# Head norms one half tile later, picks spread, and a bias table of 16 copies in a fused decoder layer

## What is computed

```
n = rmsnorm(h, g_mix)
q, k, v, qi, ki, wi, qb, kb, vb, gb, rb, uc, vc = split_proj(n @ w_in)
q, k = rmsnorm(q, q_norm_g), rmsnorm(k, k_norm_g)          # per head of 128
o_a  = attention over the top 64 (prompt) or 65 (samples) keys by indexer score,
       logits = q.k / sqrt(128) + rel_bias[rel_bucket(distance)]
o_b  = rmsnorm(gla(qb, kb, vb, log_sigmoid(gb @ w_gate_b + b) / 16)) * silu(rb)
o_c  = gelu(uc) * (w_spatial @ rmsnorm(gelu(vc)) + b_spatial)
h = h + concat(o_a, o_b, o_c) @ w_out
h = h + (silu(n2 @ w_ffn_gate) * (n2 @ w_ffn_up)) @ w_ffn_down
h = h + sigmoid(n3 @ w_ple_gate) * (p @ w_ple_proj)
```

## Time and profile before

| | |
|---|---|
| median of 3 runs | 1432.46 us (1432.43 to 1432.93) |
| profiled execution | 1431.66 us |
| its span | 1430.0 us |
| TensorE busy | 1409.9 us (99%) |
| VectorE busy | 850.1 us (59%) |
| ScalarE busy | 584.8 us (41%) |
| GpSimd busy | 111.8 us (8%) |
| moved by DMA | 237.95 MB |

### The profile page before, as it was taken

The page is one execution under the profiler, slowest core; times in us unless marked ns, Lnnn a source line. Parts: engine busy times, 40 slices in busy tenths (PEclk is TensorE's granted clock), DMA queues, the critical chain, the costliest instruction groups (busy, mean ns, idle before and its releaser), DMA issues.

```text
span 1430.0 us, 28384 instructions
## 1 busy us (share of the span) xinstructions
PE 1409.9 (99%) x10630; PEld 1383.3 (97%) x10630; DVE 850.1 (59%) x1173; ACT 584.8 (41%) x708; POOL 111.8 (8%) x160
## 2 busy tenths in 40 slices
PE   7999999999999999999999999999999999999999
PEld 7988888999999999999999999999999999999998
DVE  6568765655777555555554444555555556666654
ACT  7365554375433433333333333333333333335332
POOL 2023102210222000000000000000000001111000
PEclk9999999999999999999999999999999999999999
DMA  8766434443654545445445556554545545556553
GB/s 299 170 213 200 157 118 137 133 140 109 243 175 159 171 160 165 165 159 169 159 147 166 166 162 193 167 162 162 164 160 172 161 133 164 165 167 199 166 164 116
DMA packets 76503, 237.95 MB, mean 166 GB/s; under 512 B 13536, under 2 KB 15104, under 8 KB 76072
## 3 DMA queue, kind: packets, MB, share of 16 engines
q1 hardware_dynamic: 71136, 223.54, 48.9%
q0 software_dynamic: 3536, 11.46, 2.4%
q10 hardware_dynamic: 1784, 2.32, 1.0%
HBM read 231.35 MB, written 5.86 MB: 166 GB/s over the span
## 4 chain that ended last, share of the span: by engine, by line
PE 92%; DVE 3%; ACT 2%; DMA 2%; issue 1%; SPq 0%; DVEq 0%; ACTq 0%
PE acc L469 29%; PE acc L471 29%; PE acc L470 29%; DMA w_raw<-in_w_in 1%; DVE w_lo L435 1%; PE px L1530 1%; ACT w_hi L429 0%; PE px L1498 0%; ACT rl_s L729 0%; PE px L1479 0%; DMA proj<-in_xT 0%; PE px L469 0%; PE px L471 0%; PE px L470 0%; ACT L745 0%
## 5 line engine op out<-in xcount | busy, mean ns | idle before, releaser
L435 DVE TENSOR_TENSOR w_lo<-w_raw,w_hi 128x1024 fp32r<-128x1024 f32 (+2 forms) x448 | 510.5, 1144 | 332.4 <-ACT w_hi L429 323.6
L429 ACT ACTIVATE w_hi<-w_raw 128x1024 fp32r<-128x1024 f32 (+2 forms) x448 | 441.8, 989 | 570.2 <-PE acc L471 552.8
L469 PE MATMUL acc<-n_hi,w_hi 128*128 128x288 f32 x1664 | 492.8, 296 | 0.0
L470 PE MATMUL acc<-n_lo,w_hi 128*128 128x288 f32 x1664 | 490.9, 295 | 0.0
L471 PE MATMUL acc<-n_hi,w_lo 128*128 128x288 f32 x1664 | 489.2, 294 | 0.0
L471 PEld LDWEIGHTS acc<-n_hi,w_lo 128*128 128x128 f32 x1664 | 313.2, 188 | 0.0
L470 PEld LDWEIGHTS acc<-n_lo,w_hi 128*128 128x128 f32 x1664 | 312.2, 188 | 0.1
L469 PEld LDWEIGHTS acc<-n_hi,w_hi 128*128 128x128 f32 x1664 | 311.8, 187 | 0.1
L469 PE MATMUL acc<-x_hi,w_hi 128*128 128x288 f32 x848 | 258.4, 305 | 10.0 <-DVE w_lo L951 10.0
L470 PE MATMUL acc<-x_lo,w_hi 128*128 128x288 f32 x848 | 251.6, 297 | 0.0
L471 PE MATMUL acc<-x_hi,w_lo 128*128 128x288 f32 x848 | 250.7, 296 | 0.0
(11 more groups left out here) (262 smaller groups left out, 837.5 us busy)
## 6 DMA issues: line engine op xcount, KB each, us to landing
w_raw<-in_w_gu SPq DMA_DIRECT2D x176, 512.0 KB, 4.0
w_raw<-in_w_in SPq DMA_DIRECT2D x78, 512.0 KB, 4.1
w_raw<-in_w_down SPq DMA_DIRECT2D x64, 384.0 KB, 3.1
w_raw<-in_w_down SPq DMA_DIRECT2D x64, 320.0 KB, 3.0
w_raw<-in_w_ple SPq DMA_DIRECT2D x32, 576.0 KB, 3.8
w_raw<-in_w_out SPq DMA_DIRECT2D x32, 512.0 KB, 4.4
proj<-in_xT SPq DMA_DIRECT2D x4, 576.0 KB, 6.4
w_raw<-in_w_in SPq DMA_DIRECT2D x8, 256.0 KB, 4.8
```

The source lines that it names most:

```text
L429: nc.scalar.activation(whi[:, slot, 0:kt * P], raw[:, slot, 0:kt * P], ACT.Copy).then_inc(S("w_hi_done"), 1)
L435: nc.vector.tensor_tensor(wlo[:, slot, 0:kt * P], raw[:, slot, 0:kt * P], whi[:, slot, 0:kt * P].bitcast(F32), ALU.subtract).then_inc(S("w ...
L469: nc.tensor.matmul(out, w_h, row_of(m_hi_, k0 + k), start=first and k == 0, stop=False)
L470: nc.tensor.matmul(out, w_h, row_of(m_lo_, k0 + k), start=False, stop=False)
```

## The change

The bias table has 16 copies of each head's row in place of 128. `bias_p` is read in eight requests of 16 partitions, each from the table's beginning with another offset, and GpSimd does all the reads ahead of `mask_scores(0)`, not behind it. In the timetable `values` and `store_kv` go from half tile 26 to 27; norm 1 from 30 to 31, norm 2 from 34 to 35, norm 3 from 38 to 39 and norm 4 from 42 to 43; the squares of norms 1, 2 and 4 stay, those of norm 3 stay in 37, which is now the half tile of `softmax` 0. The scan, the attention stages and the first levels come one half tile later, `softmax_s` 1 two. Of the nine sample rounds one stands in each of half tiles 28 to 34, and the last two in 39 and 43. From level 3 (57) on all is as before.

```diff
+NCOPY = 16
-    26: [("values", 0), ("store_kv", 0), ("pick", (1, 3, 5))],
-    27: [("pick", (1, 5, 7))],
+    26: [("pick", (1, 3, 5))],
+    27: [("values", 0), ("store_kv", 0), ("pick", (1, 5, 7))],
     28: [("pick", (1, 7, 8)), ("pick_s", (0, 1))],
-    29: [("norm_sq", 1), ("pick_s", (1, 3))],
-    30: [("norm", 1), ("pick_s", (3, 4))],
-    31: [("pick_s", (4, 6))],
-    32: [("pick_s", (6, 8))],
-    33: [("norm_sq", 2), ("pick_s", (8, 9))],
-    34: [("norm", 2)],
-    35: [("scan", 0)],
-    36: [("softmax", 0)],
-    37: [("exps", 0), ("norm_sq", 3)],
-    38: [("norm", 3), ("transpose", 0)],
-    39: [("mix", 0)],
-    40: [("softmax", 1)],
-    41: [("exps", 1), ("norm_sq", 4)],
-    42: [("norm", 4), ("transpose", 1)],
-    43: [("mix", 1)],
...
+    29: [("norm_sq", 1), ("pick_s", (1, 2))],
+    30: [("pick_s", (2, 3))],
+    31: [("norm", 1), ("pick_s", (3, 4))],
+    32: [("pick_s", (4, 5))],
+    33: [("norm_sq", 2), ("pick_s", (5, 6))],
+    34: [("pick_s", (6, 7))],
+    35: [("norm", 2)],
+    36: [("scan", 0)],
+    37: [("softmax", 0), ("norm_sq", 3)],
+    38: [("exps", 0)],
+    39: [("norm", 3), ("transpose", 0), ("pick_s", (7, 8))],
+    40: [("mix", 0)],
+    41: [("softmax", 1), ("norm_sq", 4)],
+    42: [("exps", 1)],
+    43: [("norm", 4), ("transpose", 1), ("pick_s", (8, 9))],
+    44: [("mix", 1)],
...
+    50: [("exps", 3), ("transpose_s", 0)],
+    51: [("transpose", 3), ("mix_s", 0), ("softmax_s", 1), ("scale_q", 0)],
+    52: [("mix", 3), ("mix_s_back", 0), ("decays", 0)],
+    53: [("transpose_s", 1), ("level", 0)],
+    55: [("mix_s", 1), ("level", 1)],
+    56: [("mix_s_back", 1), ("level", 2)],
     57: [("level", 3)],
...
-        table = nc.dram_tensor("bias_table", [NH, P, NDIST], F32, kind="Internal").ap()
+        table = nc.dram_tensor("bias_table", [NH, NCOPY, NDIST], F32, kind="Internal").ap()
...
+            def read_bias(dst, first, rows_, keys):
+                src = bass.AP(tensor=table.tensor, offset=first, ap=[[NDIST - 1, rows_], [NCOPY * NDIST, NH], [1, keys]])
+                pool.dma_start(dst, src).then_inc(S("bias_loaded"), 16)
...
+            pool.wait_ge(S("table_written"), 16)
+            for p0 in range(0, P, NCOPY):
+                read_bias(bias_p[p0:p0 + NCOPY, :, :], DMAX - P - p0, NCOPY, SEQ)
+            read_bias(bias_s[:, 0:PAST], DMAX - PAST, NS, PAST)
+            read_bias(bias_n[:, :], DMAX, NS, NS)
             mask_scores(0)
-            pool.wait_ge(S("table_written"), 16)
-            for dst, first, rows_, keys in ((bias_p[:, :, :], DMAX - P, P, SEQ), (bias_s[:, 0:PAST], DMAX - PAST, NS, PAST),
-                                            (bias_n[:, :], DMAX, NS, NS)):
-                src = bass.AP(tensor=table.tensor, offset=first, ap=[[NDIST - 1, rows_], [P * NDIST, NH], [1, keys]])
-                pool.dma_start(dst, src).then_inc(S("bias_loaded"), 16)
             mask_scores(1)
...
-                act.dma_start(table, btab[:, :].unsqueeze(1).broadcast_to([NH, P, NDIST])).then_inc(S("table_written"), 16)
+                act.dma_start(table, btab[:, :].unsqueeze(1).broadcast_to([NH, NCOPY, NDIST])).then_inc(S("table_written"), 16)
```

More of the change, by code:

```diff
@@ L87 @@
     25: [("pick", (1, 1, 3))],
-    26: [("values", 0), ("store_kv", 0), ("pick", (1, 3, 5))],
-    27: [("pick", (1, 5, 7))],
+    26: [("pick", (1, 3, 5))],
+    27: [("values", 0), ("store_kv", 0), ("pick", (1, 5, 7))],
     28: [("pick", (1, 7, 8)), ("pick_s", (0, 1))],
-    29: [("norm_sq", 1), ("pick_s", (1, 3))],
-    30: [("norm", 1), ("pick_s", (3, 4))],
-    31: [("pick_s", (4, 6))],
-    32: [("pick_s", (6, 8))],
-    33: [("norm_sq", 2), ("pick_s", (8, 9))],
-    34: [("norm", 2)],
-    35: [("scan", 0)],
-    36: [("softmax", 0)],
-    37: [("exps", 0), ("norm_sq", 3)],
-    38: [("norm", 3), ("transpose", 0)],
-    39: [("mix", 0)],
-    40: [("softmax", 1)],
-    41: [("exps", 1), ("norm_sq", 4)],
-    42: [("norm", 4), ("transpose", 1)],
-    43: [("mix", 1)],
[L106 to L116, removed]
+    29: [("norm_sq", 1), ("pick_s", (1, 2))],
[14 more added lines that the diff above has]
+    44: [("mix", 1)],
+    45: [("softmax", 2)],
+    46: [("exps", 2), ("keys_s", 0)],
+    47: [("transpose", 2)],
+    48: [("mix", 2), ("softmax_s", 0)],
+    49: [("softmax", 3)],
+    50: [("exps", 3), ("transpose_s", 0)],
[4 more added lines that the diff above has]
+    56: [("mix_s_back", 1), ("level", 2)],
     57: [("level", 3)],
@@ L1091, in softmax @@
                 pr = prob[:, 0:NR * nk].rearrange("p (r s) -> p r s", r=NR)
-                dve.wait_ge(S("bias_loaded"), 48)
+                dve.wait_ge(S("bias_loaded"), 16 * (P // NCOPY + 2))
                 dve.wait_ge(S("sel_ready"), tt + 1)
```

## The result

The kernel after takes 1422.9 us (median of 4 executions, 1422.62 to 1422.96), the kernel before in the same comparison 1432.7 us (1432.43 to 1432.95). The ratio is 0.9932, with a 95% interval of 0.992 to 0.9943. A second comparison gave 1422.68 us and 0.993 (0.9917 to 0.9943).

A forecast was written before the change was run, and what follows sets the result against it. TensorE, busy 99%, bounds the kernel, so only its waits and slow stretch can be won: 0.64 + 0.85 + 2.06 + 2.49 + 0.75 = 6.79, plus 1.52, gives 8.3 us: 1432.46 becomes 1424.2, range 1423.0 to 1427.0.

The forecast's parts named there:

- Norms 1 and 2: TensorE's waits for VectorE's sq_lo at 134.69 and 150.74 us go: 2.06 and 2.49 us, margins 0.3 and 1.7 us.
- The clock: After norm 2's wait TensorE runs at 1.2 GHz for 3.4 us; that slow stretch costs 1.52 us and goes.
- Softmax 0 and the transposes: VectorE has the probabilities at 163.0 us, 1.0 us before TensorE's transposes; three softmax passes take 2.47 us; no wait.
- The rule that I weighed: A two-SBUF-input VectorE instruction contends with a GpSimd one reading SBUF, the later blocks; probabilities late by up to one block.
- Values: The value transposes' wait of 0.69 us at 119.15 us, for an evicted tile, goes: 0.85 us.
- norm 4: Norm 4 also gets its second half tile, so its wait at 184.57 us goes: 0.75 us.
- The ten requests: Bias reads on GpSimd, 1.1 us each, 11 us from about 51 to 62 us; effect 0, bounds -0.4 to +0.64.
- The table's write: With 16 copies the write takes 4.2 us, not 33; the relu wait at 71.07 us goes: 0.64 us.
- The rival of the starved weights: The ten requests sit on one DMA engine each time and delay weight loads from about 60 us: 1450 us; 4%.
- the median of the runs is 0.8 us above it, so 1432.46 becomes 1424.2: Final step: profiled execution 1431.66 becomes 1423.4 us, and the median's 0.8 us above it is carried over.
- VectorE arrives a round late: Rival: VectorE one sample round (1.04 us) later, 0.7 us wait at norm 1, up to 2 us: 1426; 13%.
- The wait only moves: Rival: VectorE's work from 117 to 163 us is no shorter, TensorE waits at softmax 0 and transposes: 1429.6; 4%.

The follow-up runs named there:

- after_old_picks: The kernel after with the sample rounds where they were in the old timetable, relative to the norms: 1425.88 us, ratio 0.9959.
- norms_one_half_busy: The kernel after, norms 1 and 2 one half tile behind their squares, plus 20 unread matmuls ahead of norm 1's wait: 1426.02 us, ratio 0.996.
- before_busy: The kernel before with unread matmuls filling its two long waits, 14 at norm 1 and 17 at norm 2: 1431.77 us, ratio 1.0001.
- after_values_26: The kernel after with the value transposes and the two stores back in half tile 26: 1423.53 us, ratio 0.9943.
- table_only: The kernel before with only the 16-copy bias table and its earlier reads, timetable as before: 1431.33 us, ratio 0.9992.
- before_again: The kernel before, unchanged, for more executions and one more trace: 1432.76 us median of 11 executions, ratio 1.0003.
- norms_one_half: The kernel after with norms 1 and 2 only one half tile behind their squares again: 1427.40 us, ratio 0.9964.
- before_look_2: The kernel before, unchanged, one more execution with its trace: 1433.42 us.
- before_look_1: The kernel before, unchanged, one execution with its trace: 1431.15 us.
- before_look_3: The kernel before, unchanged, one more execution with its trace: 1432.92 us.

## Why the prediction was right in its mechanism and wrong in its size

By its steps:

- *Norms 1 and 2, 4.55 us and the slow stretch of 1.52.* Right. Both follow without a wait; the traces give 2.15 + 2.90 + about 1.2 = 6.25 for my 6.07. The margins were 0.3 and 1.7 us by my count and are 0.31 and 1.5. At norm 2 the half tile (3.2 us) and the three rounds moved behind its squares (3.1) each exceed the margin, so neither could be left out. For the rounds after_old_picks shows it. For the half tile it is worked out, and norms_one_half_busy points the same way: norm 2 waits 0.26 us there, even behind a norm 1 that goes late.
- *The clock.* The price was right (1.6 us in the traces of the two runs, 1.38 in their medians), the reason that it could be added was not one that I gave. In the kernel before it is worth nothing (before_busy). It counts only because VectorE no longer sets the pace behind it.
- *Softmax 0 and the transposes.* Margin 1.0 by my count, 0.9 in the trace. The three passes took 2.10 us (157.56 to 159.66) where I had used 2.47; the difference is the bias addition, 0.73 us for 1.10. In both kernels GpSimd's distances run beside it. Before, it started at 160.52, amid the first of them (159.58 to 161.08); after, at 157.56, 0.2 us before the first one's end and ahead of the second one's start at 157.71. The rule that I weighed (the Trainium skill, SBUF — State Buffer, section "Who interferes with whom") fits these two, in the direction of a gain. The same addition takes 0.68 us at 189.48 in after, where GpSimd is idle, so the neighbour cost it 0.42 us before and 0.05 after. Norm 3 and mix 0 gained 0.5 us that I had left at nothing; that this comes from the earlier probabilities is argued, no run tests it.
- *Values, 0.85, and norm 4, 0.75.* Right: 0.87 and 0.82; after_values_26 gives 0.6 to 0.85 us of the values back.
- *The ten requests, 0.* Right. They take GpSimd 5.4 us and not 11, and weight loads land in 6.1 us beside them. The rival of the starved weights falls.
- *The table's write, 0.64.* One number for a cost that varies. I read it from the one wait of 0.48 us in the earlier trace rows. In the five traces of the kernel before the write costs 0 to 2.3 us; by the medians the smaller table alone is worth 0.54 us (table_only).
- *The step that failed* is "the median of the runs is 0.8 us above it, so 1432.46 becomes 1424.2". I took the distance between the profiled execution and the median for a property of the measurement, and carried it over to the changed kernel. It was time that the kernel before spends in some executions and spent less of in the profiled one: waits behind late weight loads beside the table's write. The change shortens that write from 35 us to 5, and after's profiled execution is no quicker than its median (1422.96 and 1422.9). The 0.8 us was also large for the kernel before itself: it came from three executions, and against the median of all 73, 1431.99, the profiled one is only 0.33 us quicker. With the offset counted as part of the table's term, as 0.64 + 0.8 = 1.44, the same sum ends at 1432.46 - 9.1 = 1423.4; the other 0.4 us to 1422.9 and the norm 3 and mix gain of 0.5 are about the same thing.

Of the rivals, *VectorE arrives a round late* (1426) did not happen in after. That after_old_picks, at 1425.88, meets its price is luck: there VectorE is three rounds late and not one, at norm 2 and the two stages behind it and not at norm 1, whose squares stand ahead of the moved rounds. *The wait only moves* describes the kernel before (before_busy, before_again) and not the one after. The range began at 1423.0 for want of a case in which the change gains more than its waits.

Open stays why the late loads differ from execution to execution. The Trainium skill, DMA: Bandwidth & Descriptors, section "Why a DMA increments its semaphore by 16 and not by 1", has the write go over 8 engines, and each weight load needs all 16, so a load would end with those eight; the packets' 41.5% agree with eight, but no run here moved the write to others. It wasn't tried either whether fewer copies than 16, or the same 128 with larger packets, behave otherwise. And no execution of the kernel before above 1434 us has a trace: that they wait for late loads too is inferred from those at 1432.92 and 1433.42.

## What to carry to other kernels

When the profiled execution is quicker than the median and the executions spread, the gap is time of the kernel that the trace doesn't show: look for what is slowed without being waited for in that trace (here loads landing in 16 us and not 6, whose slack was nearly used up), and give it a term of its own that a change to it takes along. Where a second engine is full from stage to stage, count margins in its queue and not waits one by one: a wait or a clock loss that is taken away comes back at the next stage until that queue itself is rearranged. 

## What the runs showed of the hardware

- A wait of TensorE of 1.83 to 2.71 us could be followed by a stretch of some 3.4 us at the 1.2 GHz level, worth 1.38 us in the medians of norms_one_half and norms_one_half_busy. Not every one was: behind norm 1's wait of 1.83 to 1.90 us the clock fell in three traces (before_again, before_look_2, table_only) and stayed at 1.00 in three (before, before_look_1, before_look_3), where it fell behind norm 2's 2.33 us instead. A wait of 2.00 us at 83.8 us (before_look_2) had no slow stretch behind it. Matmuls whose result nobody reads kept the clock at 1.00.
- While one DMA of 128 copies of a 1552-byte row, from 8 partitions, ran (its packets move from 45 to about 80 us in the trace of before), 512 KB loads of another queue landed in about 16 us in place of 4 to 6. With 256 copies this lasted 70 us. Meanwhile the DMA moved only 113 GB/s from 50 to 56 us, against 161 in the kernel after.
- A VectorE addition of two 128x512 inputs took 1.10 us when it began 0.56 us before the end of a GpSimd operation, 0.73 us when it began 0.2 us before that end and ahead of the next operation, and 0.68 us with GpSimd idle.
- GpSimd issued eight DMA requests of constant addresses in 4.22 us, 0.53 us each; key pages, whose number it reads first, cost it about 1.1 us.
